# The output projection of a two-block layer on one core: plain products, and products of block sums for 12 of 16 feature tiles

## The chip, the cores and the metric

The kernel runs on one core of one Trainium2 chip. The metric is the device time of one execution in microseconds. PE is TensorE's matmul side, PEld its weight loads, DVE is VectorE, ACT is ScalarE, POOL is GpSimd and SP is SyncE, which here only issues DMAs.

## The reference, cut to what matters

Two blocks follow each other on x of 512 positions by 2048 features (batch 1). The first is a mixer of attention and a gated recurrence; the second has three attention branches, each brought up to 2048 features, gated and summed. The change touches only the last line:

```
merged = g_a * (oa @ w_up_a) + g_b * (ob @ w_up_b) + g_c * (oc @ w_up_c)
x = x + merged @ w_o          # (512 x 2048) @ (2048 x 2048)
```

## The kernel before

All activations are held transposed: features on the 128 partitions in 16 tiles (KT = 16), the 512 positions along the free side. A product is one output tile of 128 features by 512 positions, summed over the 16 input tiles in one bank. float32 accuracy comes from splitting both operands in two fp32r parts, hi (a rounded copy) and lo (what is left): each input tile takes three matmuls, hi by hi (L824), weight hi by activation lo (L825), weight lo by activation hi (L826), each 128x128 weights by 512 columns.

**Weights** come in items of up to 1024 columns (`weights()`, 438 of them, ITEMS). SP loads item after item into a ring of three buffers `wraw` (L2255), ACT makes `whi` (`split`, L1125), POOL makes `wlo` (`remainder`, L2127), and PE's `part` waits for it. `w_o` gives 32 items, two for each output tile (input tiles 0 to 7 and 8 to 15, LOW and HIGH).

**Order.** Every engine runs the same walk, `in_order`, over its own program, so each engine's instructions stand in the order of that walk. `Beat` has three lines of side work ("core", "post", "slow"): each line holds generators, and each slot (one after four input tiles of a part) lets each line take one step. `drain` takes steps until the named lines are empty, with no matmul of a part between them.

**The last stages.** `mix(2, 6)` makes the merged activations: for each output tile nb a gate (16 input tiles), then a short product over six tiles (`thin`), then on DVE the evacuation `bank * gate` (L1711) and the sum with the other two branches (L1715) into `y[nb]`, which counts `mg2`. A gate's own side work is three ACT functions, one on DVE (L1742), one on ACT and a copy on POOL (L2185). Beside it `put` makes hi (ACT, L1262) and lo (DVE L1659 for three of four tiles, POOL L2145 for the fourth) of each finished `y[k]`; these are the moving operands "m" of the last product. Tiles 0 to 7 are ready when the last product begins, tiles 8 to 15 follow beside its first 96 matmuls (two output tiles' LOW halves stand first for that). For each output tile SP loads `x1s[nb]` (`out_load`, L2366), DVE adds bank and `x1s` (L1722, `kind == "last"`), and SP stores the result (L2352). The last tile is evacuated in two halves of 256 columns, the second stored from ACT's queue.

Of the kernel before, what the change touches and what calls it, by code (L numbers as in the profile page):

```python
# [97 lines left out]
def weights():  # L98
# [159 lines left out]
class Memory:  # L258
    def __init__(self, nc, ctx):
# [112 lines left out]

        self.cmb = {1: self.cmb[:, 0:256], 2: self.rt[1], 3: self.cmb}

    def dst(self, kind, i=0, *_):
# [36 lines left out]
class Signals:  # L412
    def __init__(self, nc, ctx):
# [56 lines left out]

        self.u, self.ua, self.mg2, self.out = sem("u"), sem("ua"), sem("mg2"), sem("out")


# [8 lines left out]
def in_order(beat, do):  # L482
# [170 lines left out]
    def mx(k):  # L653
        return "m", k, "y", k, ("mg2", k + 1), k % 4 != 0

    def mx_early():
        beat.add("slow", puts(*([mx(k)] for k in range(EARLY, 8))))

    for nb, _ in enumerate(mix(2, 6)):
        if nb < EARLY:  # L660
            beat.add("slow", puts([], [], [mx(nb)]))
    beat.drain("core", "post", "slow")
    beat.add("slow", puts(*([mx(k), mx(k + 1)] for k in range(8, 16, 2))))
    do["out_load"](0)
    do["out_load"](1)
    second = (beat.open(), beat.open())
    for n, ks in enumerate((LOW, HIGH)):
        for nb, bank in enumerate(second):
            do["part"]("m", ks, bank, n == 0, n == 1)
            if n:  # L670
                close("last", bank, nb)
    for nb in range(2, KT):
        do["out_load"](nb)
        full("m", "last", nb)
    do["end"]()
# [41 lines left out]
def tensor_program(nc, M, S, beat):  # L717
# [115 lines left out]
    def out(kind, bank, *at):  # L833
        if kind in BY_ACT:
            free[bank] = (S.eva, n.up("eva"))
        elif kind in BY_DVE:
            free[bank] = (S.evd, n.up("evd"))
        else:
            free[bank] = {"x1": (S.x1, n["x1"] + 1), "mix": (S.u, n["mix"] + 1), "last": (S.out, n["last"] + 1)}[kind]
# [258 lines left out]
    def h2(k):  # L1098
        put("h", k, None, 0, None, on_vector(k))

    in_order(beat, dict(
        setup=setup, mem=mem, mem_kv=nothing, mem_norm=lambda: rest(3), mem_turn=mem_turn, ada=nothing, h=h,
        begun=begun, hv=hv, gates=lambda g: rest(GATE_STEPS), hg=hg, attend=attend, window=window, put=put, x_load=nothing, h2=h2, index=index,
        topk=lambda: rest(48), mix_load=nothing, out_load=nothing, end=nothing,
        part=part, out=out, posts=dict(
# [6 lines left out]
def scalar_program(nc, io, M, S, beat):  # L1112
# [144 lines left out]
    def put(x, k, src, i, mark, on_dve):  # L1257
        act.wait_ge({"y": S.y, "o": S.o, "mg2": S.mg2, "nrm": S.nrm}[mark[0]], mark[1])
        act.wait_ge(S.item, beat.used[home(x, k) if home(x, k)[0] != "t" else ("o", 5)])
        if x == "y" and home(x, k)[0] == "o":  # L1260
            act.wait_ge(S.adm, 2 * KT)
        e.activation(M.pair[x][0][k], src[i] if isinstance(src, list) else {"y": M.y, "ost": M.ost}[src][i],  # L1262
                     ACT.Copy).then_inc(S.phi)

    def out(kind, bank, *at):
# [12 lines left out]
        if kind == "x1":  # L1278
# [3 lines left out]
            e.activation(M.sqt if i else M.sqa, M.y[nb], ACT.Square).then_inc(S.xsqa)  # L1282
        if kind == "last" and at[0] == KT - 1:
            act.wait_ge(S.out, KT + 1)
            e.dma_start(io["out"][KT - 1, :, LAST[1]], M.u[1][:, LAST[1]]).then_inc(S.ust[1], 16)
        if kind == "ik":
# [237 lines left out]
    def h2(k):  # L1524
        act.wait_ge(S.x1, NB.index(k) + 1)
        act.wait_ge(S.item, beat.used["h", k])
        e.activation(M.pair["h"][0][k], M.y[k], ACT.Copy, scale=M.c("norm_g2", k, 1)).then_inc(S.phi)

    def nothing(*at):
        pass  # L1530
# [3 lines left out]
        gates=lambda g: rest(GATE_STEPS), hg=hg, attend=attend, window=window, put=put, x_load=nothing, h2=h2, index=index, topk=lambda: rest(48), mix_load=nothing,  # L1534
        out_load=nothing, end=nothing, part=part, out=out, posts=dict(
            decay=decay, hq=silu("hq"), hz=silu("hz"),
# [10 lines left out]
def vector_program(nc, M, S, beat):  # L1547
# [128 lines left out]
    def out(kind, bank, *at):  # L1676
# [28 lines left out]
        elif kind == "mix":  # L1705
# [6 lines left out]
            if branch == 2:  # L1712
                dve.wait_ge(S.u, 32 + nb + 1)
                dve.wait_ge(S.lb[nb % 2], 16 * (8 + nb // 2 + 1))
                e.tensor_tensor(M.y[nb], M.u[nb % 2], M.lb[nb % 2], ALU.add).then_inc(S.mg2)  # L1715
        elif kind == "last":
            nb = at[0]
            dve.wait_ge(S.lb[nb % 2], 16 * (16 + nb // 2 + 1))
            dve.wait_ge(S.ust[nb % 2], 16 * (16 + nb // 2))
            dve.wait_ge(S.item, beat.item)  # L1720
            for w in LAST if nb == KT - 1 else (slice(0, T),):
                e.tensor_tensor(M.u[nb % 2][:, w], src[:, w], M.lb[nb % 2][:, w], ALU.add).then_inc(S.out)  # L1722

# [372 lines left out]
    def h2(k):  # L2096
# [6 lines left out]
        else:  # L2103
            n.up("plp")

    def nothing(*at):
        pass

    in_order(beat, dict(
        setup=setup, mem=mem, mem_kv=nothing, mem_norm=mem_norm, mem_turn=lambda: rest(2), ada=ada, h=h, begun=begun, hv=nothing,  # L2110
        gates=gates, hg=hg, attend=attend, window=window, put=put, x_load=nothing, h2=h2, index=index, topk=topk, mix_load=nothing, out_load=nothing, end=nothing,
        part=part, out=out, posts=dict(
# [6 lines left out]
def gpsimd_program(nc, M, S, beat):  # L2119
# [106 lines left out]
    def h2(k):  # L2226
        phi = n.up("phi")
        if not on_vector(k):
            pool.wait_ge(S.phi, phi)
            pool.wait_ge(S.hb, [nb for nb in NB if not on_vector(nb)].index(k) + 1)  # L2230
            e.tensor_tensor(M.pair["h"][1][k], M.hb[k], M.pair["h"][0][k].bitcast(F32), ALU.subtract).then_inc(S.plp)  # L2231

    def nothing(*at):
        pass

    def idle(steps):
# [11 lines left out]
def sync_program(nc, io, M, S, beat):  # L2248
# [90 lines left out]
    def out(kind, bank, *at):  # L2339
        if kind == "x1":  # L2340
            i, nb = at
            sp.wait_ge(S.x1, i + 1)
            e.dma_start(io["x1s"][nb], M.y[nb]).then_inc(S.x1s, 16)
        elif kind == "mix" and at[0] < 2:
            branch, nb = at
            sp.wait_ge(*((S.u, nb + 1) if branch == 0 else (S.ua, nb + 1)))
            e.dma_start(io["mgs"][nb], M.u[nb % 2]).then_inc(S.ust[nb % 2], 16)
        elif kind == "last":
            nb = at[0]
            sp.wait_ge(S.out, nb + 1)  # L2350
# [11 lines left out]

    def out_load(nb):
        sp.wait_ge(*((S.out, nb - 1) if nb > 1 else (S.mg2, 16)))
        sp.wait_ge(S.x1s, 16 * KT)
        e.dma_start(M.lb[nb % 2], io["x1s"][nb]).then_inc(S.lb[nb % 2], 16)  # L2366

    def end():
        for b in range(2):
            sp.wait_ge(S.ust[b], 16 * (24 + b))  # L2370

# [3 lines left out]
    def idle(steps):  # L2375
# [4 lines left out]
        gates=gates, hg=hg, attend=attend, window=window,  # L2380
        put=nothing, x_load=x_load, h2=nothing, index=idle(3), topk=idle(48), mix_load=mix_load, out_load=out_load,
        end=end, part=part, out=out, posts=dict(
# [110 lines left out]
```

## Time and profile before

| | us |
|---|---|
| median of three runs | 2596.74 (2596.69 to 2596.79) |
| the profiled execution | 2597.67 |
| its span, first to last instruction | 2596.4 |
| busy: PE / PEld / DVE / ACT / POOL | 2580.0 / 2077.6 / 1028.8 / 1082.6 / 1140.5 |

The page gives busy time of each engine, the chain of waits followed back from the last instruction (97% PE, 3% DVE), and groups of instructions by line. A row of the timeline reads: start in us from the span's start, duration in us, engine, line, operation, output<-input, count, and in brackets the idle time before and what ended it. A matmul's duration runs to its modelled end, and the next begins before that: the pace is read from starts.

### The profile page before, as it was taken

The page shows a single profiled execution, that of the slowest core. Times are in us where ns is not written, and L with a number is a line of the kernel's source. Part 1 is how long each engine was busy: PE and PEld are TensorE (multiplying, and loading weights), DVE is VectorE, ACT ScalarE, POOL GpSimd, SP SyncE. Part 2 cuts the span into 40 slices and gives each one's busy share as a digit, 9 for nine tenths or more (in the row PEclk, how much of TensorE's full clock was granted, in tenths as well). Part 3 has the DMA queues.
Part 4 walks back from the last instruction along what each step waited for, and adds up shares of the span by engine and source line. Part 5 has one row for each costly group of instructions (what it writes and reads, how often), then busy time and mean ns, then how long its engine had stood idle before and what let it go on. Part 6 is the DMA issues. An engine that isn't in the chain of part 4 may idle for free.

```text
span 2596.4 us, 33094 instructions
## 1 busy us (share of the span) xinstructions
PE 2580.0 (99%) x13414; PEld 2077.6 (80%) x13414; DVE 1028.8 (40%) x1622; ACT 1082.6 (42%) x1769; POOL 1140.5 (44%) x580
## 2 busy tenths in 40 slices
PE   8999999999999999999999999999999999999999
PEld 3778777877888888888888888888888888888887
DVE  3963444435444421344785343334333223312300
ACT  4334344444445432344444444444444444333311
POOL 0014444343434454543454444445555556554543
PEclk9999999999999999999999999999999999999999
DMA  9953333233333244422222333333333333333443
GB/s 398 389 176 111 106 99 113 82 118 102 122 102 114 86 134 146 126 89 81 90 81 86 106 99 100 103 100 106 102 107 119 120 110 111 119 108 115 148 145 104
DMA packets 97785, 322.84 MB, mean 124 GB/s; under 512 B 10977, under 2 KB 13025, under 8 KB 93025
## 3 DMA queue, kind: packets, MB, share of 16 engines
q1 hardware_dynamic: 92016, 301.16, 34.9%
q10 hardware_dynamic: 5616, 19.56, 2.0%
q8 instruction: 107, 1.75, 0.3%
q14 instruction: 46, 0.37, 0.0%
HBM read 303.90 MB, written 16.78 MB: 124 GB/s over the span
## 4 chain that ended last, share of the span: by engine, by line
PE 97%; DVE 3%; DMA 0%; ACT 0%; issue 0%; POOL 0%; SPq 0%; DVEq 0%; ACTq 0%
PE bank L824 28%; PE bank L826 28%; PE bank L825 28%; PE bank L767 2%; PE bank L1019 1%; PE bank L1008 1%; PE bank L939 1%; DVE TA L1610 1%; PE bank L1002 1%; PE bank L973 1%; DVE first L1610 1%; DVE wlo L1593 0%; PE bank L1055 0%; PE bank L1070 0%; PE bank L788 0%; PE bank L866 0%
## 5 line engine op out<-in xcount | busy, mean ns | idle before, releaser
L2127 POOL TENSOR_TENSOR wlo<-wraw,whi 128x1024 fp32r<-128x1024 f32 (+3 forms) x420 | 970.2, 2310 | 1318.4 <-ACT whi L1125 1318.2
L824 PE MATMUL bank<-Hhi,whi 128*128 128x512 f32 x2720 | 1093.6, 402 | 0.2 <-POOL Hlo L2231 0.2
L826 PE MATMUL bank<-Hhi,wlo 128*128 128x512 f32 x2720 | 1061.9, 390 | 0.0
L825 PE MATMUL bank<-Hlo,whi 128*128 128x512 f32 x2720 | 1060.5, 390 | 0.0
L1125 ACT ACTIVATE whi<-wraw 128x1024 fp32r<-128x1024 f32 (+3 forms) x438 | 440.5, 1006 | 685.9 <-PE bank L826 647.2
L824 PEld LDWEIGHTS bank<-Hhi,whi 128*128 128x128 f32 x2720 | 511.0, 188 | 113.8 <-issue 9.9
L826 PEld LDWEIGHTS bank<-Hhi,wlo 128*128 128x128 f32 x2720 | 510.6, 188 | 109.2
L825 PEld LDWEIGHTS bank<-Hlo,whi 128*128 128x128 f32 x2720 | 511.4, 188 | 103.5 <-issue 2.2
L824 PE MATMUL bank<-Ohi,whi 128*128 128x512 f32 x320 | 127.9, 400 | 0.0
L826 PE MATMUL bank<-Ohi,wlo 128*128 128x512 f32 x320 | 124.8, 390 | 0.0
L825 PE MATMUL bank<-Olo,whi 128*128 128x512 f32 x320 | 124.6, 389 | 0.0
L1689 DVE TENSOR_TENSOR TA<-bank,rows 128x512 f32<-128x512 f32 x48 | 33.1, 690 | 201.7 <-PE bank L826 201.7
L1795 DVE TENSOR_TENSOR TR<-TA,TR 128x512 fp32r<-128x512 f32 x38 | 51.2, 1347 | 77.5 <-ACT TR L1352 77.5
L1742 DVE SCALAR_TENSOR_TENSOR TA<-TA,par 128x512 f32<-128x512 f32 x48 | 46.7, 972 | 71.7 <-ACT TA L1302 69.2
L1742 DVE SCALAR_TENSOR_TENSOR TA<-TA 128x512 f32<-128x512 f32 x32 | 60.1, 1879 | 33.3 <-ACT TA L1302 33.3
L1722 DVE TENSOR_TENSOR TA<-bank,TA 128x512 f32<-128x512 f32 (+1 forms) x17 | 11.1, 660 | 151.6 <-PE bank L826 151.6
L824 PEld LDWEIGHTS bank<-Ohi,whi 128*128 128x128 f32 x320 | 60.1, 188 | 13.3 <-issue 1.4
L825 PEld LDWEIGHTS bank<-Olo,whi 128*128 128x128 f32 x320 | 60.1, 188 | 13.1 <-issue 1.2
L826 PEld LDWEIGHTS bank<-Ohi,wlo 128*128 128x128 f32 x320 | 60.1, 188 | 12.6
L1274 ACT ACTIVATE TA<-bank 128x512 f32<-128x512 f32 x49 | 29.0, 592 | 97.2 <-PE bank L826 97.2
L1689 DVE TENSOR_TENSOR Y<-bank,rows 128x512 f32<-128x512 f32 x45 | 30.9, 687 | 92.7 <-PE bank L826 86.1
L767 PE MATMUL bank<-wmem,HF 128*128 128x512 f32 x128 | 59.6, 617 | 8.1 <-ACT HF L1156 8.1
(272 smaller groups left out, 2733.9 us busy)
## 6 DMA issues: line engine op xcount, KB each, us to landing
wraw<-in_w_in SPq DMA_DIRECT2D x293, 512.0 KB, 3.5
TA<-in_w_ada SPq DMA_DIRECT2D x22, 1024.0 KB, 17.1
first<-in_w_ada SPq DMA_DIRECT2D x32, 512.0 KB, 4.5
wraw<-in_w_out SPq DMA_DIRECT2D x32, 512.0 KB, 3.5
wraw<-in_w_o SPq DMA_DIRECT2D x32, 512.0 KB, 3.5
first<-in_w_ada SPq DMA_DIRECT2D x10, 1024.0 KB, 14.0
wmem<-in_w_mem ACTq DMA_DIRECT2D x16, 512.0 KB, 9.4
wraw<-in_w_beg ACTq DMA_DIRECT2D x16, 512.0 KB, 7.7
```

The lines of the kernel that those rows point to most:

```text
L767: m = e.matmul(M.banks[MEM_BANKS[2 * kv + tt]], M.memf[k][:, tt * P:(tt + 1) * P], w[:, kv * T:(kv + 1) * T], start=k == 0, stop=k == KT - 1)
L824: e.matmul(out, hi[:, c], xhi[k], start=first and j == 0, stop=False)
L825: e.matmul(out, hi[:, c], xlo[k], start=False, stop=False)
L826: m = e.matmul(out, lo[:, c], xhi[k], start=False, stop=last and end)
L939: m = e.matmul(M.banks[bank][keys:keys + G, i * w:(i + 1) * w], k[:, i * P + keys:i * P + keys + G], q[:, i * P + queries:i * P + queries ...
L1125: e.activation(M.whi[b][:, 0:w], M.wraw[b][:, 0:w], ACT.Copy).then_inc(S.hi)
L1274: e.activation(M.dst(kind, *at), src, ACT.Copy).then_inc(S.eva)
L1610: e.tensor_tensor_reduce(out=w, in0=w, in1=M.cb, scale=gain, scalar=begin, op0=ALU.mult, op1=ALU.add, accum_out=total).then_inc(S.adv)
L1689: e.tensor_tensor(dst, src, M.rows, ALU.mult).then_inc(S.evd)
L1742: e.scalar_tensor_tensor(out=M.t2, in0=x, scalar=bias, in1=M.t1, op0=ALU.min, op1=ALU.subtract).then_inc(S.t2)
L1795: e.tensor_tensor(M.sql, M.W2["SQ"], M.sqh.bitcast(F32), ALU.subtract).then_inc(S.sql)
L2127: e.tensor_tensor(M.wlo[b][:, 0:w], M.wraw[b][:, 0:w], M.whi[b][:, 0:w].bitcast(F32), ALU.subtract).then_inc(S.lo)
```

## The change

Input tiles are paired, six pairs (`CROSSED`: 0 and 1, 2 and 3, 4 and 5, 10 and 11, 12 and 13, 14 and 15), output tiles are paired (8 groups), and positions are halved (LEFT, RIGHT, 256 each). Each two by two block product is made in seven products of block sums in place of eight. The four input tiles 6 to 9 (`PLAIN`) stay plain, n1 and n2, 12 matmuls of 512 columns each; a product is 18 matmuls of 256 columns. The order is `SEQ`; the plain parts of group g + 1 stand ahead of the products of group g.

- Sums of activations: four DVE operations of 256 columns for each pair (`sums`), hi of 256, 512 and 1024 columns on ACT, lo of 256 and 512 on POOL and of 1024 on DVE (`forms`).
- Sums of weights: p5, p6, p7 and p3 each need a DVE sum of 768 columns (`low`), then hi of 768 columns on ACT (`high`), then lo: on DVE for p1, p5, p6, p7, p3, on POOL for p2, p4, n1, n2. All are made three products ahead (LOOK), in four buffers.
- Banks: p1, p6, p7, p4 accumulate in one bank R; after each DVE takes the running sum (`take`, 256 columns, bank and SBUF in), and PE waits for that before the next of them. p5 and p3 do so in Q. p2 adds to the plain sum in X. DVE ends a group with two additions of 512 columns.
- DVE, in a step of product q, first takes product q - 1, then makes what product q + 3 needs.
- The last plain weights no longer pass through the ring; `begin` makes the first three hi and lo after the walk's last `thin`, behind `forms(4)`. SP issues four 768-column loads, two 512-column loads, two `x1s` loads and two stores for each group, in place of four 1024-column loads, two `x1s` loads and two stores.
- `w_o` is laid out anew by the host, in the order of the tiles.

```diff
+CROSSED = ((0, 1), (2, 3), (4, 5), (10, 11), (12, 13), (14, 15))
+PLAIN = range(6, 10)
+STRIP = len(CROSSED) * P
+PRODUCTS = ("p1", "p5", "p6", "p2", "p7", "p3", "p4")
+SEQ = [(0, "n1"), (0, "n2")]
+for pair in range(GROUPS):
+    SEQ += [(pair + 1, x) for x in ("n1", "n2") if pair < GROUPS - 1] + [(pair, x) for x in PRODUCTS]
+LO_BY_POOL = ("n1", "n2", "p2", "p4")
+LOOK = 3
...
     def mx_early():
-        beat.add("slow", puts(*([mx(k)] for k in range(EARLY, 8))))
+        beat.add("slow", do["forms"](3))
+        beat.add("slow", puts([mx(6), mx(7)], [mx(8), mx(9)]))
+        beat.add("slow", do["begin"]())
+        beat.add("core", rest(2))
+        beat.add("core", do["sums"](4))
+        beat.add("core", do["forms"](4))
...
     beat.drain("core", "post", "slow")
...
+    beat.add("slow", do["sums"](5))
+    beat.add("slow", do["forms"](5))
+    beat.drain("slow")
+    for q in range(len(SEQ)):
+        do["last"](q)
...
# PE
+    def last(q):
+        pe.wait_ge(S.lop if what in LO_BY_POOL else S.lod, lows(q, what in LO_BY_POOL))
...
+        elif what in ("p1", "p5"):
...
+                pe.wait_ge(S.took, 6 * g - (what == "p5"))
+        elif what != "p2":
+            pe.wait_ge(S.took, 6 * g + {"p6": 1, "p3": 2, "p7": 3, "p4": 4}[what])
...
+            e.matmul(out, hi[:, c], xhi, start=start and j == 0, stop=False, skip_group_check=True)
+            e.matmul(out, hi[:, c], xlo, start=False, stop=False, skip_group_check=True)
+            m = e.matmul(out, lo[:, c], xhi, start=False, stop=True, skip_group_check=True)
...
# ACT
+        if q == 0:
+            act.wait_ge(S.lo, len(ITEMS))
...
+        else:
+            act.wait_ge(S.item, len(ITEMS) + q - 3)
+        if what in ("p5", "p6", "p7", "p3"):
+            act.wait_ge(S.wsum, 4 * g + ("p5", "p6", "p7", "p3").index(what) + 1)
...
+        e.activation(M.hi4[q % 4][:, 0:at.shape[-1]], at, ACT.Copy).then_inc(S.hi)
...
# DVE
+        elif what == "p7":
+            e.tensor_tensor(a21, a21, a11, ALU.add).then_inc(S.wsum)
...
+        e.tensor_tensor(lo, src, M.hi4[q % 4][:, 0:STRIP].bitcast(F32), ALU.subtract).then_inc(S.lod)
...
+        elif what == "p6":
+            e.tensor_tensor(x1[:, RIGHT], R, x1[:, RIGHT], ALU.add).then_inc(S.took)
...
+    def last(q):
+        if q:
+            take(q - 1)
+        low(q + LOOK)
```

## Rows read from the trace of the kernel before

**Rows 1.** Windows view, the last product: us, then busy time (instructions) of each engine.

```profile
core 0: us, PE busy (x) PEld busy (x) DVE busy (x) ACT busy (x) POOL busy (x), PEclk, DMA share, GB/s
2419.30:2593.60 174.30, 174.30 (x770) 144.07 (x768) 21.74 (x24) 35.99 (x38) 76.46 (x33) 1.00 0.41 131
```

**Rows 2.** Timeline, two L824 matmuls of 512 columns, three matmuls apart.

```profile
2479.92 0.39 PE L824 MATMUL bank<-Hhi,whi 128*128 128x512 f32 x1
...
2480.60 0.39 PE L824 MATMUL bank<-Hhi,whi 128*128 128x512 f32 x1
```

**Rows 3.** Timeline, two fp32r matmuls of 256 columns and the one behind them.

```profile
1230.22 0.28 PE L1088 MATMUL bank<-Olo,Ohi 128*128 128x256 f32 x1
...
1230.34 0.28 PE L1089 MATMUL bank<-Olo,Ohi 128*128 128x256 f32 x1
...
1230.45 0.40 PE L824 MATMUL bank<-Hhi,whi 128*128 128x512 f32 x1
```

**Rows 4.** Timeline, twenty weight loads of 128 columns with short matmuls between them.

```profile
240.43 2.42 PEld L973 LDWEIGHTS bank<-TA,Y 128*128 128x128 f32 x20
```

**Rows 5.** Source view, DVE: duration min/median/max in ns, first and last start, forms.

```profile
L1593 DVE TENSOR_TENSOR wlo<-wraw,whi x18: 1218/1222/1226, 71.2 to 165.6; 128x1024 fp32r<-128x1024 f32 x18
L1659 DVE TENSOR_TENSOR Hlo<-Y,Hhi x13: 678/1092/2234, 913.2 to 2431.1; 128x512 fp32r<-128x512 f32 x13
L1711 DVE TENSOR_TENSOR TA<-bank,TA x48: 683/692/693, 1412.4 to 2420.2; 128x512 f32<-128x512 f32 x48
L1722 DVE TENSOR_TENSOR TA<-bank,TA x17: 415/692/693, 2436.0 to 2594.1; 128x512 f32<-128x512 f32 x15, 128x256 f32<-128x256 f32 x2
```

**Rows 6.** Lines view by form: ACT's hi of 768 columns.

```profile
L1125 ACT ACTIVATE whi<-wraw 128x768 fp32r<-128x768 f32 x32 | 27.0, 845 | 47.1 <-PE bank L826 47.1
```

**Rows 7.** Source view, POOL's lo of 512 columns, and of weights from 1700 us on.

```profile
L2145 POOL TENSOR_TENSOR TR<-Y,TR x1: 1296/1296/1296, 2274.9 to 2274.9; 128x512 fp32r<-128x512 f32 x1
...
L2127 POOL TENSOR_TENSOR wlo<-wraw,whi x172: 732/2399/2902, 1698.6 to 2578.6; 128x1024 fp32r<-128x1024 f32 x125, 128x768 fp32r<-128x768 f32 x32, 128x256 fp32r<-128x256 f32 x12, 128x512 fp32r<-128x512 f32 x3
```

**Rows 8.** Timeline, POOL: a copy of 512 columns, and the lo of 768.

```profile
2403.62 0.61 POOL L2185 COPY TA<-TA 128x512 f32<-128x512 f32 x1
2406.98 1.85 POOL L2127 TENSOR_TENSOR wlo<-wraw,whi 128x768 fp32r<-128x768 f32 x1 [2.75 <-ACT whi L1125]
```

**Rows 9.** Timeline, POOL and DVE side by side.

```profile
2416.72 2.41 POOL L2127 TENSOR_TENSOR wlo<-wraw,whi 128x1024 fp32r<-128x1024 f32 x1 [1.67 <-ACT whi L1125]
2417.05 2.62 DVE L1715 TENSOR_TENSOR Y<-TA 128x512 f32<-128x512 f32 x1
```

**Rows 10.** Timeline, an item's last matmul and those who waited for it.

```profile
2484.45 0.39 PE L826 MATMUL bank<-Hhi,wlo 128*128 128x512 f32 x1
...
2484.94 1.06 ACT L1125 ACTIVATE whi<-wraw 128x1024 fp32r<-128x1024 f32 x1 [4.38 <-PE bank L826]
2484.98 0.69 DVE L1722 TENSOR_TENSOR TA<-bank,TA 128x512 f32<-128x512 f32 x1 [10.19 <-PE bank L826]
...
2486.08 2.40 POOL L2127 TENSOR_TENSOR wlo<-wraw,whi 128x1024 fp32r<-128x1024 f32 x1 [3.04 <-ACT whi L1125]
```

**Rows 11.** Timeline near the start: ACT hands to DVE, and DVE to a waiting PE.

```profile
76.95 0.72 ACT L1239 ACTIVATE Hhi<-Y,par 128x512 fp32r<-128x512 f32 x1 [6.57 <-DVE Y L1616]
...
77.71 0.75 DVE L1630 SCALAR_TENSOR_TENSOR Hlo<-Y,par,Hhi 128x512 fp32r<-128x512 f32 x1 [0.79 <-ACT Hhi L1239]
...
78.56 0.47 PE L788 MATMUL bank<-whi,Hhi 128*128 128x512 f32 x1 [1.16 <-issue]
```

**Rows 12.** Timeline ahead of the last product and its first matmul.

```profile
2414.41 0.61 ACT L1262 ACTIVATE Hhi<-Y 128x512 fp32r<-128x512 f32 x1
...
2419.40 0.39 PE L824 MATMUL bank<-CKhi,whi 128*128 128x512 f32 x1
```

**Rows 13.** Timeline, the last evacuation.

```profile
2593.78 0.76 DVE L1722 TENSOR_TENSOR TA<-bank,TA 128x256 f32<-128x256 f32 x2 [10.19 <-PE bank L826]
```

**Rows 14.** DMA view: KB each, median us from issue to landing.

```profile
wraw<-in_w_o SPq DMA_DIRECT2D x32, 512.0 KB, 3.5
```

More of the change, by code:

```diff
@@ L838, in out @@
         else:
-            free[bank] = {"x1": (S.x1, n["x1"] + 1), "mix": (S.u, n["mix"] + 1), "last": (S.out, n["last"] + 1)}[kind]
+            free[bank] = {"x1": (S.x1, n["x1"] + 1), "mix": (S.u, n["mix"] + 1)}[kind]
             n.up(kind)
@@ L1103, in tensor_program @@
         begun=begun, hv=hv, gates=lambda g: rest(GATE_STEPS), hg=hg, attend=attend, window=window, put=put, x_load=nothing, h2=h2, index=index,
[L1104 removed]
+        topk=lambda: rest(48), mix_load=nothing, end=nothing, sums=lambda j: rest(1), forms=lambda j: rest(2),
+        begin=lambda: rest(3), last=last,
         part=part, out=out, posts=dict(
@@ L1534, in scalar_program @@
         gates=lambda g: rest(GATE_STEPS), hg=hg, attend=attend, window=window, put=put, x_load=nothing, h2=h2, index=index, topk=lambda: rest(48), mix_load=nothing,
-        out_load=nothing, end=nothing, part=part, out=out, posts=dict(
+        end=nothing, sums=lambda j: rest(1), forms=forms, begin=begin, last=last,
+        part=part, out=out, posts=dict(
             decay=decay, hq=silu("hq"), hz=silu("hz"),
@@ L1713, in out @@
                 dve.wait_ge(S.u, 32 + nb + 1)
+                if nb == 14:
+                    dve.wait_ge(S.fd, 4)
                 dve.wait_ge(S.lb[nb % 2], 16 * (8 + nb // 2 + 1))
                 e.tensor_tensor(M.y[nb], M.u[nb % 2], M.lb[nb % 2], ALU.add).then_inc(S.mg2)
[L1716 to L1722, printed above, removed]
     def gates(g):
@@ new lines, in last @@
+    def last(q):
+        if q == 0:
+            x1_load(0)
+            x1_load(1)
+            sp.wait_ge(S.fp, 8)
+            sp.wait_ge(S.fd, 4)
+            sp.wait_ge(S.item, len(ITEMS) + 1)
+            for what in ("a21", "a22", "a12"):
+                block(0, what)
+            a_blocks(1)
+            n_blocks(2)
+        elif q > 2 and SEQ[q][0] and SEQ[q] == (SEQ[q][0], "p1"):
+            g = SEQ[q][0]
+            store(g - 1)
+            if g < GROUPS - 1:
+                x1_load(g + 1)
+                a_blocks(g + 1)
+            if g < GROUPS - 2:
+                n_blocks(g + 2)
+        if q == len(SEQ) - 1:
+            store(GROUPS - 1)
@@ L2380, in sync_program @@
         gates=gates, hg=hg, attend=attend, window=window,
-        put=nothing, x_load=x_load, h2=nothing, index=idle(3), topk=idle(48), mix_load=mix_load, out_load=out_load,
+        put=nothing, x_load=x_load, h2=nothing, index=idle(3), topk=idle(48), mix_load=mix_load, sums=idle(1), forms=forms,
+        begin=idle(3), last=last,
         end=end, part=part, out=out, posts=dict(
```

320 lines of the change are left out of this document (280 added, 40 removed).

## Prediction

> **What bounds the kernel now.** I read the windows view over the last product first, then PE's timeline inside it, then the durations of every kind of operation that the change adds, wherever the trace has one. In the last product PE is busy for all of its 174.30 us, at full granted clock, while DVE is busy for 21.74, ACT for 35.99 and POOL for 76.46 [rows 1]. The pace of a 512-column matmul is (2480.60 - 2479.92) / 3 = 0.2267 us [rows 2], so 768 of them are 174.1 us. No other engine shows there; fewer columns on PE is the way to less time, until another engine's chain is longer than PE's.
>
> **What PE saves.** A group (two output tiles) has 96 matmuls of 512 columns now: 21.76 us. Afterwards it has 24 of 512 columns (5.44 us) and 7 x 6 x 3 = 126 of 256. Two such, each with its own weight load, took 1230.45 - 1230.22 = 0.23 us [rows 3]: 0.115 each. Bounds: 256 columns at 2.4 GHz are 0.107; adding what a 512-column matmul takes over its own 0.213, 0.013, gives 0.120. A row of twenty weight loads ran at (2.42 - 0.19) / 19 = 0.117 [rows 4], 0.19 being one load, so the load does not rule 0.115 out, and 0.115 is measured on the very form. A product is then 18 x 0.115 = 2.07 us, a group 5.44 + 14.49 = 19.93, all eight 159.4: 14.7 us under now. A group breaks even at (21.76 - 5.44) / 126 = 0.1295.
>
> One page of the Trainium skill speaks against it: TensorE: Matmul & The Clock Gate, section "The mechanism", says that a weight load overlaps matmuls in flight only where their row groups differ. By that rule, every load of this kernel would lie bare. [Rows 3] show full-height loads hidden even under 256 columns, so it has next to no weight in the sum.
>
> **What DVE, ACT and POOL now have to do in step with PE.** Prices: a DVE operation on two SBUF tiles is 0.69 us for 512 columns and 1.22 for 1024 [rows 5], so 0.96 for 768; a take of 256 columns 0.42, an addition from a bank of 512 columns 0.69 [rows 5]; independent DVE operations overlap by 2 x 0.42 - 0.76 = 0.08 [rows 13]. ACT's hi of 768 is 0.85 [rows 6], POOL's lo 1.85 for 768 and 1.30 for 512 [rows 8, 7]. ACT to DVE is 0.04, and I take 0.03 to 0.04 for the way back; a waiting PE starts 0.10 after DVE's end, and its first matmul is 0.08 longer [rows 11]. DVE starts 0.14 after an item's last matmul ends [rows 10]; with 0.28 for a 256-column matmul [rows 3] that is 0.30 after the next product has begun.
>
> DVE's work per group is 9 x 0.96 + 6 x 0.42 + 2 x 0.69 = 12.5 us of 19.9, not a bound by share. But p6, p7, p3 and p5 each want sum, hi, lo in turn (0.96 + 0.03 + 0.85 + 0.03 + 0.96 = 2.83), and DVE stands still while ACT makes hi. PE may not begin p7 before DVE has taken p6 out of bank R, and in DVE's order that take stands behind the weights of p3. From the end of p1: take p1 starts at 0.30, sum of p7 0.64 to 1.60, hi to 2.48, lo to 3.47, take p5 to 3.81, sum of p3 3.73 to 4.69, hi to 5.57, lo to 6.56, take p6 to 6.90, PE at 7.00. PE itself needs 3 x 2.07 = 6.21 for p5, p6, p2. PE waits 0.79, with the longer first matmul 0.87, in each of eight groups.
>
> **The port.** DVE operations with two SBUF inputs range from 0.68 to 2.23 us, those that read a bank from 0.683 to 0.693 [rows 5]; a 0.69 one that began 0.33 after a POOL operation took 2.62 and ended 0.54 after it [rows 9]. I read that as: such an operation and a POOL operation take turns. In the chain, hi of p2 follows that of p6; counted from the group's start (0.30, take p4 0.42, addition 0.03 + 0.69, two rounds of 0.88 + 0.91 + 0.96) lo of p6 ends at 6.9, POOL's lo of p2 runs from there to 8.7, and the sum of p7 wants to start at 5.44 + 2.07 + 0.64 = 8.15. It waits 0.55. So p7 waits 1.42 in seven groups (the last has no plain parts in its walk, DVE is ahead there by one turn, 0.87): 10.8 us. Bounds: nothing, or the whole 1.85 instead of 0.55, 9 us more.
>
> **The last group** has no plain parts between p4 of group 6 and its own p1. Three products ahead, DVE makes p5 (from 0.3 after p3 of group 6 began: take, sum, hi, lo to 3.5), takes p3 (0.3), adds 512 columns (0.7), makes p6 (2.7), and only then takes p4, 7.5 us after p3 began, when PE has been done for 7.5 + 0.1 - 4.14: 3.6 us with the restart.
>
> **The start.** The first plain lo, POOL's, stands behind lo of m7, the gate's copy, lo of m9 and two of `forms(4)`. The m conversions stand where ACT now converts at 2414.41 [rows 12]; hi of m7 ends about 1.1 later, POOL starts at 2415.6 and needs 4 x 1.30 + 0.73 + 0.61 = 6.5 [rows 7, 8]: 2422.1, where PE is free at 2419.40 [rows 12]. That is 2.8 with the hand-over; DVE's m8 and y15 take turns with it, at most 2 x 0.69 and one 1.22 more. I take 3.7, between 2.8 and 5.4; nothing excludes less if ACT comes earlier. The four plain parts (10.9 us) cover `sums(5)` and `forms(5)`; DVE is then about 0.7 late at the first take, added once. During `mix` the new sums stand beside a PE that needs 15 us per tile (66 matmuls), and 2.9 us of DVE and 2.1 of ACT for each pair of tiles are hidden there; if they are not, it shows as idle PE before 2419.
>
> **DMA.** The weights' bytes are the same and x and output too, 131 GB/s now [rows 1]; a 512 KB load lands 3.5 us after issue [rows 14], and each block is issued most of a group ahead. Free; SP waits only for steps that lie behind. If the first group's three blocks, issued after the first plain part, were later than 10 us, p5 would wait.
>
> **The end.** The last evacuation is one of 0.42 in place of two in 0.76 [rows 13]: -0.35.
>
> **Sum.** 159.4 + 10.8 + 3.6 + 0.7 + 3.7 = 178.2 against 174.1: +4.1, at the end -0.35: +3.8. On the profiled execution's 2597.67 that is 2601.5; the median of the runs is 0.93 below it, so I forecast 2600.5. A nanosecond of pace is worth only 0.4 us, since DVE's chain stays: 0.107 to 0.120 gives -3.3 to +2.0.
>
> **Rivals.**
> - *DVE keeps up*: the chain to p7 is 7.0 against 6.2, a matter of ten hand-overs and five durations interpolated or taken elsewhere. If they overlap better, p7 waits little, the start costs 1.5, and what is left is 159.4 + 3.6 + 1.5 = 164.5: about 2587. For it: DVE's share of 63%. Against: every term has its row, and the order is strict.
> - *The port decides (slower)*: POOL has four passes a group, 6.3 us, and any that starts ahead of a sum or lo in p7's chain adds up to 1.85. It makes the change slower by 0.2% once it adds 0.2 us more to a group than I count; a full pass gives 3.8 + 7 x 1.3 = +13: 2610. For it: DVE waits of 2 us at 512 columns in [rows 5, 9]. Against: in my order POOL's lo of p4, n1 and n2 falls where DVE is idle.
> - *The load sets the pace*: 126 loads in a row at 0.130 make +5.6 on the stage where I have -0.4: +10, 2606. [Rows 4], at 0.117, speak against.
> - *Loads not hidden in a long row*: 0.115 + 0.117 [rows 3, 4] for each of 1008 matmuls, with 43.5 for the plain ones 277 in place of 174: 2700. [Rows 3] leave it a chance of 1%. It is what the rule of the Trainium skill's page TensorE: Matmul & The Clock Gate, section "The mechanism", would make of this stage.
>
> **Chances.** The forecast's case 0.46, DVE keeps up 0.25, port 0.20, pace 0.08, unhidden 0.01. 0.2% is 5.2 us, about what a measurement of this kernel can tell from no change. The forecast's case has 0.36 within it, 0.08 above and 0.02 below; the first rival is faster, the others slower: 0.27, 0.36, 0.37. Its own range is 2595 to 2606; the range over all cases 2586 to 2611.
>
> **What would show it.** Right: starts of 256-column matmuls 0.113 to 0.118 apart; seven gaps on PE of about 1.4 us ahead of p7, released by DVE's take; one of 3.6 late; one of some 3.7 at 2419, released by POOL. In DVE's rows sums of 0.96, some stretched by 0.5. Wrong: no idle PE at p7 (then the first rival), DVE operations near 2.8 us (the second), a pace over 0.12 (the third), or waits for DMAs.

## The result and the profile after

The changed kernel takes 2611.17 us (median of four runs, 2610.45 to 2612.29) beside 2596.76 for the kernel before on the same chip: a ratio of 1.0055, with a 95% interval of 1.0043 to 1.0067. That is 14.4 us more, 0.55%, where 3.8 more were forecast; it lies 0.2 us above the range and on its slow side. The profiled execution took 2610.45, its span is 2609.1, so between the two profiled spans there are 12.7 us. The runs of the changed kernel spread over 1.8 us, those of the kernel before over 0.3.

The page's head, each engine's busy time and instructions:

```profile
span 2609.1 us, 34342 instructions
PE 2576.8 (99%) x13846; PEld 2094.0 (80%) x13846; DVE 1135.1 (44%) x1762; ACT 1107.2 (42%) x1815; POOL 1132.0 (43%) x590
```

PE is busy for only 3.2 us less than the 2580.0 of before, in a longer span, and DVE for 106 more. The windows view over the last product shows where. The rows are the start, the middle, the last group's first 8 us and the whole stage:

```profile
core 0: us, PE busy (x) PEld busy (x) DVE busy (x) ACT busy (x) POOL busy (x), PEclk, DMA share, GB/s
2418.50:2431.00 12.50, 8.87 (x27) 6.74 (x27) 10.73 (x8) 4.30 (x8) 10.52 (x9) 0.73 0.38 119
2447.00:2585.00 138.00, 130.57 (x948) 123.80 (x949) 80.00 (x107) 42.16 (x55) 39.95 (x25) 1.00 0.40 134
2585.00:2593.00 8.00, 4.52 (x27) 4.35 (x26) 3.80 (x6) 1.58 (x2) 1.93 (x1) 0.79 0.17 66
2418.70:2606.90 188.20, 171.17 (x1202) 160.77 (x1200) 113.13 (x144) 55.71 (x74) 57.94 (x37) 0.97 0.37 124
```

Beside [rows 1] there are three new things. PE idles: 17 us of the stage. The granted clock is not 1.00 any more at two places, 0.73 at the start and 0.79 in the last group. And PE is busy for 171.17 where the forecast's own matmuls came to 159.4 (a busy time holds the modelled ends and the slow matmuls too). The stage takes 187.9, from 2418.77 (behind the last matmul of `mix`) to 2606.7, in place of 174.1.

**The pace.** PE's timeline inside p2 of group 1:

```profile
2466.18 0.28 PE L1199 MATMUL bank<-TR,w3lo 128*128 128x256 f32 x1
...
2466.54 0.28 PE L1199 MATMUL bank<-FX,w3lo 128*128 128x256 f32 x1
```

Three matmuls take 0.36: 0.120 each, and that is what most of the 1008 show. [Rows 3] had 0.115.

**The wait ahead of p7**, the same stretch of all engines: DVE makes the sum of p3 (L2295), ACT its hi, DVE its lo (L2300) and only then takes p6 (L2318).

```profile
2465.68 0.95 DVE L2295 TENSOR_TENSOR first<-first 128x768 f32<-128x768 f32 x1
...
2466.72 1.58 ACT L1662 ACTIVATE whi<-first 128x768 fp32r<-128x768 f32 x2 [2.35 <-DVE first L2295]
...
2467.62 0.28 PE L1199 MATMUL bank<-Hlo,w3lo 128*128 128x256 f32 x1
2467.67 0.96 DVE L2300 TENSOR_TENSOR wlo<-first,whi 128x768 fp32r<-128x768 f32 x1 [1.04 <-ACT whi L1662]
...
2468.55 0.42 DVE L2318 TENSOR_TENSOR TA<-bank,TA 128x256 f32<-128x256 f32 x1
...
2469.11 0.36 PE L1197 MATMUL bank<-TR,whi 128*128 128x256 f32 x1 [1.21 <-DVE TA L2318]
```

From 2467.62 to 2469.11 are 1.49, less one step of pace 1.37, and 0.08 more for the longer first matmul. DVE stood still for 1.04 between its sum and its lo, 0.84 for hi and 0.20 for the two hand-overs. Six groups are like this; the first waits 2.12 and the last 0.77. Why DVE is behind is told by the source views of its sum for p7 (L2291) and of the take:

```profile
L2291 DVE TENSOR_TENSOR first<-first x4: 948/1562/1570, 2461.9 to 2593.5; 128x768 f32<-128x768 f32 x4
```

```profile
L2318 DVE TENSOR_TENSOR TA<-bank,TA x8: 416/418/419, 2446.5 to 2599.6; 128x256 f32<-128x256 f32 x8
...
  PE bank L1197: 9.9, 8
```

The sum takes 1.56 where POOL's lo of p2 runs beside it, and 0.948 in the last group, where nothing does. PE waited for the take 8 times.

**The two long waits and what stands behind them.** The start:

```profile
2418.54 0.39 PE L891 MATMUL bank<-Ohi,wlo 128*128 128x512 f32 x1
2422.56 0.80 PE L1197 MATMUL bank<-Hhi,w3hi 128*128 128x512 f32 x1 [3.63 <-POOL w3lo L2492]
2423.15 0.63 PE L1198 MATMUL bank<-Hlo,w3hi 128*128 128x512 f32 x1
2423.58 0.63 PE L1199 MATMUL bank<-Hhi,w3lo 128*128 128x512 f32 x1
```

A wait of 4.02 - 0.23 = 3.79, released by POOL. Then the matmuls begin 0.43 apart in place of [rows 2]'s 0.227: the 1.2 GHz level. That goes on for 13 of them, 2.9 us in all.

The last group:

```profile
2585.64 0.28 PE L1199 MATMUL bank<-Hhi,w3lo 128*128 128x256 f32 x1
...
2588.84 0.41 DVE L2333 TENSOR_TENSOR TA<-TA,bank 128x256 f32<-128x256 f32 x1
...
2589.40 0.55 PE L1197 MATMUL bank<-TR,whi 128*128 128x256 f32 x1 [3.48 <-DVE TA L2333]
...
2590.18 0.41 PE L1197 MATMUL bank<-TR,whi 128*128 128x256 f32 x1
```

A wait of 3.76 - 0.12 = 3.64, and 13 matmuls of 256 columns, most of them 0.213 apart, 1.4 us more. Here the Trainium skill's page TensorE: Matmul & The Clock Gate has a section, "HAM oscillation — how this bites in real kernels", by which a wait inside a kernel can put TensorE back to half its clock, so that the work behind it starts slow; these rows agree, and the prediction had no term for it.

The whole stage is then 1008 x 0.120 + 192 x 0.2267 = 164.5 for the matmuls, 2.20 + 6 x 1.46 + 0.85 = 11.8 for the waits ahead of p7, 3.8 and 3.6 for the two long ones, 2.9 + 1.4 = 4.3 for the clock: 188.0, where 187.9 were measured.

**What sets the time at the start.** That sum says what PE did, not what each part of it cost. The critical view, which follows the work that ended last, leaves PE for 28 us here: it goes from the last matmul of `mix` to DVE, through DVE's and ACT's operations one behind the other, and comes back to PE with p7 of the first group.

```profile
2418.70 0.24 PE bank L891
2419.03 0.70 DVE TA L1858
...
2446.54 0.43 DVE TA L2318
2447.11 0.36 PE bank L1197
```

In all that time DVE waits only for ACT (five times 1.0 to 1.1), never for PE. Several of its operations are long beside POOL's: 2.29 and 1.87 for lo of 1024 and 768 columns and 2.27 for the sum of p7, which take 1.23, 0.96 and 0.95 elsewhere in the stage. So the wait of 3.79, the 2.9 us of slow matmuls behind it and the first group's pace did not lengthen this execution: without them PE would have waited for the same take for longer. In the last group it is otherwise. There the same view goes through the slow matmuls of p1, and their 1.4 us count.

### The profile page after: what moved, and what is told of

Same layout as the page of the kernel before. It is cut to its first block, busy times and chain, and to the rows that moved or that the text cites. A ratio compares the mean times of both kernels' runs of the same rounds, so it can differ in the third digit from the quotient of the medians.

```text
span 2609.1 us, 34342 instructions
## 1 busy us (share of the span) xinstructions
PE 2576.8 (99%) x13846; PEld 2094.0 (80%) x13846; DVE 1135.1 (44%) x1762; ACT 1107.2 (42%) x1815; POOL 1132.0 (43%) x590
## 4 chain that ended last, share of the span: by engine, by line
PE 94%; DVE 4%; ACT 1%; issue 1%; DMA 0%; POOL 0%; DVEq 0%; SPq 0%; ACTq 0%
PE bank L889 26%; PE bank L891 25%; PE bank L890 25%; PE bank L832 2%; PE bank L1084 1%; PE bank L1073 1%; PE bank L1197 1%; PE bank L1199 1%; PE bank L1198 1%; PE bank L1004 1%; DVE TA L1757 1%; PE bank L1067 1%; PE bank L1038 1%; DVE first L1757 1%; ACT whi L1662 1%
## 5 line engine op out<-in xcount | busy, mean ns | idle before, releaser
L2370 POOL TENSOR_TENSOR wlo<-wraw,whi 128x1024 fp32r<-128x1024 f32 (+3 forms) x388 | 894.6, 2306 | 1218.9 <-ACT whi L1227 1218.8
L889 PE MATMUL bank<-Hhi,whi 128*128 128x512 f32 x2544 | 1025.1, 403 | 0.2 <-POOL Hlo L2474 0.2
L891 PE MATMUL bank<-Hhi,wlo 128*128 128x512 f32 x2544 | 993.4, 390 | 0.0
L890 PE MATMUL bank<-Hlo,whi 128*128 128x512 f32 x2544 | 992.1, 390 | 0.0
L1227 ACT ACTIVATE whi<-wraw 128x1024 fp32r<-128x1024 f32 (+3 forms) x406 | 406.5, 1002 | 554.4 <-PE bank L891 515.5
L889 PEld LDWEIGHTS bank<-Hhi,whi 128*128 128x128 f32 x2544 | 477.9, 188 | 106.9 <-issue 9.9
L891 PEld LDWEIGHTS bank<-Hhi,wlo 128*128 128x128 f32 x2544 | 477.5, 188 | 102.4
L890 PEld LDWEIGHTS bank<-Hlo,whi 128*128 128x128 f32 x2544 | 478.3, 188 | 96.8 <-issue 2.2
L1465 ACT ACTIVATE TA<-bank,par 128x512 f32<-128x512 f32 x39 | 26.9, 689 | 97.4 <-PE bank L932 97.4
## 6 DMA issues: line engine op xcount, KB each, us to landing
TA<-in_w_ada SPq DMA_DIRECT2D x22, 1024.0 KB, 17.1
```

The costliest lines, as they stand in the source:

```text
L889: e.matmul(out, hi[:, c], xhi[k], start=first and j == 0, stop=False)
L890: e.matmul(out, hi[:, c], xlo[k], start=False, stop=False)
L891: m = e.matmul(out, lo[:, c], xhi[k], start=False, stop=last and end)
L1227: e.activation(M.whi[b][:, 0:w], M.wraw[b][:, 0:w], ACT.Copy).then_inc(S.hi)
L1465: e.activation(W["R"], M.bST, ACT.Ln, scale=1.0 / k, bias=M.eps).then_inc(S.ln)
L2370: e.tensor_tensor(M.wlo[b][:, 0:w], M.wraw[b][:, 0:w], M.whi[b][:, 0:w].bitcast(F32), ALU.subtract).then_inc(S.lo)
```

## The experiments

The theory when the runs were planned, by PE's own sum: against the forecast, 5 us come from a pace of 0.120, which is PE's own in a long row, and 4.3 from the clock that falls behind PE's waits of over 3 us; the waits themselves are as priced. (That the first 2.9 of the 4.3 lie beside DVE's chain was not in it.) Rivals: the pace is 0.115 and something around (ports, DVE, POOL) makes it 0.120; the slow matmuls belong to the kernel's start and end, or to its new form, and not to the waits.

**Pace alone.** The kernel before, each of its last product's matmuls cut in two of 256 columns; its DVE, ACT, POOL and DMA work stays. This kernel does not compute the right product: both halves of a bank are begun with `start`, and its output is off by 0.177, about what the first input tile missing from one half would give (an estimate, the root of 1/32; which terms are missing was not shown). Number and shape of PE's matmuls are as said, and the reading rests on those.

```diff
-            e.matmul(out, hi[:, c], xhi[k], start=first and j == 0, stop=False)
...
+            for w in (slice(0, 256), slice(256, 512)) if x == "m" else (slice(0, T),):
+                begins = first and j == 0
+                e.matmul(out[:, w], hi[:, c], xhi[k][:, w], start=begins, stop=False, skip_group_check=True)
...
```

> The kernel before, with each group of three matmuls of the last product made for 256 columns and then for the other 256, weights loaded anew for each: 1536 matmuls of 256 columns with nothing else changed and nothing to wait for. Theory (a long row of such matmuls runs at 0.120 each, the pace that the changed kernel shows): the stage is 1536 x 0.120 = 184.3 us in place of 174.1: +10.2, 2607. Rival (0.115 to 0.116, the pace of the isolated pairs before, and 0.120 is what DVE's and POOL's work beside it makes of it): 177.4: +3.3, 2600.

Measured: 2607.59 (2607.11 to 2607.62), ratio 1.0040 (1.0024 to 1.0056). Windows view, and PE's timeline:

```profile
2440.00:2580.00 140.00, 140.00 (x1169) 140.00 (x1168) 8.30 (x12) 25.48 (x24) 57.51 (x25) 1.00 0.41 136
```

```profile
2500.00 0.28 PE L826 MATMUL bank<-CKhi,whi 128*128 128x256 f32 x1
...
2500.36 0.28 PE L826 MATMUL bank<-CKhi,whi 128*128 128x256 f32 x1
```

No wait, full clock, 0.120 per matmul with DVE busy for 6% of the time. POOL is busy for 41% of it, but the starts are 0.120 apart where POOL stands idle as well as beside its operations. So the pace is that of the row itself, and the rival of 0.115 falls. 1536 matmuls at 0.120 are 184.3, 10.2 over 174.1; the run is 10.4 over its control.

**The order on DVE.** In every group the take of p6 is put ahead of lo of p3.

```diff
-        low(q + LOOK)
+        if SEQ[q][1] == "p2":
+            low(q + LOOK - 1, (1,))
+        low(q + LOOK, (0,) if SEQ[q][1] == "p6" else (0, 1))
...
```

The second argument of `low` names its steps: 0 is the sum, 1 is the lo.

> The changed kernel, with DVE's lo of p3 moved behind its take of p6; nothing else. Theory (p7's wait is DVE's order: the take stands behind work that PE needs only two products later): the seven gaps of 1.38 us and the one of 2.1 ahead of p7 go, with the 0.08 of each restart; -10.5: 2600.7. Rival (the port: POOL's lo of p2 keeps the sum of p7 waiting): gaps of at least 0.6 stay ahead of p7, -6 at most: 2605.

Measured: 2600.59 (2599.72 to 2602.27, ten runs), ratio 1.0013 (1.0004 to 1.0023). 10.6 us of the 14.4 are gone. PE's windows row has 133.86 busy of 135; what is left is the first group's wait, 1.30:

```profile
2440.00:2575.00 135.00, 133.86 (x987) 127.94 (x987) 84.49 (x112) 45.12 (x59) 41.65 (x26) 1.00 0.41 137
```

So the order made those waits, as the prediction's chain had it. In the last group the wait has grown from 3.64 to 4.6, since PE now comes there earlier than DVE does:

```profile
2580.31 0.55 PE L1197 MATMUL bank<-TR,whi 128*128 128x256 f32 x1 [4.46 <-DVE TA L2337]
```

**The port.** Only 8 of 768 columns of p2's lo are made, so that POOL is out of the way of p7's sum; PE makes the same matmuls, with what the buffer held before in the other 760.

```diff
-        w = src.shape[-1]
+        w = src.shape[-1] if what != "p2" else 8
+        src = src[:, 0:w]
```

> The changed kernel, with POOL's lo of p2 made for 8 of 768 columns in every group, so that the rest of that lo is left out of the result's terms; order and waits unchanged. Theory (DVE's sum of p7 stands still while POOL makes lo of p2): the sum of p7 takes 0.96 in place of 1.56, and each gap ahead of p7 shrinks by 0.6: seven groups, -4: 2607. Rival (no turn-taking, the 1.56 has another cause): the gaps stay at 1.38, 2611.

Measured: 2606.87 (2606.43 to 2607.11), ratio 1.0038 (1.0023 to 1.0052). Source view of the sum, and a wait ahead of p7:

```profile
L2291 DVE TENSOR_TENSOR first<-first x4: 948/949/950, 2462.1 to 2589.5; 128x768 f32<-128x768 f32 x4
```

```profile
2467.84 0.28 PE L1199 MATMUL bank<-Hlo,w3lo 128*128 128x256 f32 x1
2468.71 0.36 PE L1197 MATMUL bank<-TR,whi 128*128 128x256 f32 x1 [0.60 <-DVE TA L2318]
```

The sum is back at 0.949, by 0.61, and the wait falls from 1.38 to 0.76, by 0.62. DVE and POOL do take turns, and each turn that stands in p7's chain reaches PE in full. The Trainium skill's page SBUF — State Buffer, section "Who interferes with whom", has this rule (an operation with two SBUF inputs against a POOL operation that reads SBUF: one blocks), and the trace agrees, 0.6 a group.

The first group shows it more strongly. There the sum of p7 falls from 2.27 to 0.95, and p7 begins 1.30 us earlier (2445.81 for 2447.11). Something else stands there too: behind a wait of only 1.95 ahead of that p7, 15 matmuls ran slow, beginning 1.5 us after the wait's end.

**The start.** `begin`'s first plain lo is put ahead of `forms(4)` in the walk.

```diff
+        def first_of_begin():
+            yield
+            next(begin)
+            yield
...
-        beat.add("core", rest(2))
+        beat.add("core", first_of_begin())
```

> The changed kernel, with the first plain lo (and its hi) made one slot of the gate's HIGH half earlier, ahead of m7, m9 and forms(4) in POOL's order. Theory (POOL's queue makes the start wait, and the wait lets TensorE's clock fall): the 3.8 us gap ahead of the first matmul goes, the granted clock in 2418 to 2431 stays at 1.0 in place of 0.73, the plain matmuls are 0.227 apart and not 0.427; 6.7 us are won there, and some 1.5 given back as waits for lo of n2 and for forms(5): 2611.2 - 5.2 = 2606. Rival (the low clock comes with the change of stage, new banks and new operands, and not with the gap): the gap goes, the first 13 matmuls still stand 0.427 apart: 2609.

Measured: 2610.18 (2609.54 to 2612.16), ratio 1.0050 (1.0033 to 1.0067): 1 us less than the changed kernel, which is within the spread of the runs, and 4 more than expected. The wait of 3.8 is gone and the matmuls behind it run at 0.227, but POOL has the same passes to make and is late for the next two plain products:

```profile
2421.53 0.39 PE L1206 MATMUL bank<-Hhi,w3lo 128*128 128x512 f32 x1
2422.91 0.50 PE L1204 MATMUL bank<-Hhi,whi 128*128 128x512 f32 x1 [0.98 <-POOL wlo L2499]
...
2428.27 0.39 PE L1206 MATMUL bank<-Hhi,wlo 128*128 128x512 f32 x1
2431.66 0.79 PE L1204 MATMUL bank<-Hhi,whi 128*128 128x512 f32 x1 [3.00 <-POOL wlo L2499]
```

1.15 and 3.16. Behind 1.15 the matmuls stay at full pace; behind 3.16 they are slow again, in another place and another group than in the changed kernel. A wait on a queue that is full was moved, not removed. And it could not have given 5 us: p7 of the first group began at 2446.48 in place of 2447.11, again after a wait for DVE's take, of 1.98. Most of those 0.6 us was lost again in the last group, where in this execution 28 matmuls ran slow behind the wait of 3.64, for 2.8 us.

**The last group.** DVE takes p4 of group 6 ahead of what it makes for p6 of group 7.

```diff
-        if q:
+        if q and SEQ[q] != (GROUPS - 1, "p1"):
             take(q - 1)
+        if SEQ[q] == (GROUPS - 2, "p4"):
+            take(q)
```

> The changed kernel, with DVE's take of p4 of group 6 moved ahead of the weights of p6 of group 7; nothing else. Theory (the wait of 3.64 us ahead of p1 of group 7 is this order, and the clock falls behind it): a gap of some 0.8 stays, and the 14 matmuls that ran 0.1 longer run at full clock: -2.8 - 1.5 = -4.3: 2606.9. Rival (the slow matmuls after the gap are not from the gap): -2.8: 2608.4.

Measured: 2611.34 (2610.07 to 2611.42), ratio 1.0052 (1.0037 to 1.0067): nothing gained where 4.3 were expected. The wait ahead of p1 fell to 0.78, but DVE's work was only put off, and PE met it at p7:

```profile
2596.41 0.28 PE L1199 MATMUL bank<-Hlo,w3lo 128*128 128x256 f32 x1
2599.53 0.36 PE L1197 MATMUL bank<-TR,whi 128*128 128x256 f32 x1 [2.85 <-DVE TA L2318]
...
2600.26 0.41 PE L1199 MATMUL bank<-CKhi,wlo 128*128 128x256 f32 x1
2600.48 0.41 PE L1197 MATMUL bank<-cbr,whi 128*128 128x256 f32 x1
```

A wait of 3.0, and 0.6 us behind its end the pace goes from 0.12 to 0.21.

This trace also differs from the changed kernel's in a place that the edit does not touch. At the start only 7 matmuls ran slow and PE came to the first group's p7 1.2 us earlier (2443.63 for 2444.87). It gained nothing by it: DVE's take stands where it stood, and so does p7.

```profile
2446.54 0.42 DVE L2318 TENSOR_TENSOR TA<-bank,TA 128x256 f32<-128x256 f32 x1
...
2447.10 0.55 PE L1197 MATMUL bank<-TR,w3hi 128*128 128x256 f32 x1 [3.20 <-DVE TA L2318]
```

The wait is 3.35 in place of 2.12, and behind it 12 matmuls ran slow, 1.3 us, which the changed kernel's trace does not have. So some of what the edit may have gained is hidden by the clock's own spread, and what it is worth by itself is not settled by this run.

**All three together.**

> The three moves together. Theory: what is left of the stage is PE at 0.120 per 256-column matmul, 164.5 us, with some 3 us of small waits: 2611.2 - 5.2 - 10.5 - 4.3 = 2591.2, under the 2596.8 of the kernel before. Rival (with PE ahead by that much, DVE's chain of p5, p6, p7 and p3 shows somewhere else in each group, as waits for lo or for the takes): gaps of about 1 us per group come back elsewhere: 2599.

Measured: 2596.44 (2595.72 to 2598.49, ten runs), ratio 0.9997 (0.9988 to 1.0006): no slower and no faster than the kernel before, and 5 above what was expected. The start still has its 1.15 and 3.16 and the slow matmuls behind, and the last group waits of 1.75 and 1.0. Windows, the start and the middle:

```profile
2418.50:2440.00 21.50, 17.52 (x85) 14.33 (x84) 16.99 (x15) 6.55 (x10) 12.64 (x9) 0.92 0.55 201
2440.00:2575.00 135.00, 134.87 (x995) 128.91 (x994) 84.30 (x113) 45.12 (x59) 40.50 (x25) 1.00 0.41 137
```

With take and lo exchanged and less lost in the last group, the middle has no wait left but 0.13.

**The fourth plain lo early too**, on top of these three, made before the sums and forms of the last pair:

```diff
+        high(3)
+        yield
...
     def last(q):
-        high(q + LOOK)
+        if q:
+            high(q + LOOK)
...
```

That is ACT's part; POOL's is the same with `low`.

> The three moves together, and the hi and lo of n2 of group 1 made ahead of sums and forms of the last pair. Theory (the 3.2 us wait ahead of n2 of group 1 and the clock's fall behind it come from that order): both go, 3.2 + 1.8 us, and up to 1.6 come back as a wait for lo of p1: 2596.4 - 3.4 = 2593.0, below the kernel before by more than noise. Rival (DVE's late sums of the last pair only move the wait to p1, and it stays above 3 us there with the clock's fall): 2596.

Measured: 2596.15 (2595.38 to 2597.74, eleven runs), ratio 0.9997 (0.9988 to 1.0006). The wait of 3.16 and the clock's fall are gone:

```profile
2418.50:2440.00 21.50, 18.02 (x99) 14.98 (x98) 17.49 (x15) 6.40 (x10) 12.12 (x9) 1.00 0.57 201
2440.00:2575.00 135.00, 133.26 (x980) 127.14 (x978) 84.33 (x114) 45.12 (x59) 40.51 (x25) 1.00 0.41 137
2575.00:2595.00 20.00, 15.57 (x126) 15.22 (x126) 11.97 (x18) 4.01 (x5) 3.91 (x2) 1.00 0.15 53
```

But DVE, 17.5 of 21.5 us busy at the start, is now late for products of the first group: seven waits of 0.6 to 1.8 stand in the stage, five up to 2444.23 and two in the last group, 8.2 us in all. Expected was 2593. By the critical view the chain at the start runs through DVE and ACT from 2419.2 to 2444.2, where p7 of the first group begins; that is 0.5 us earlier than with the three moves alone (2444.23 for 2444.75). The wait of 3.16 and the 1.7 us of slow matmuls behind it are gone, and only those 0.5 us have come of it.

**Waits of several lengths, and nothing else.** The kernels above show slow matmuls only behind waits, but in each the surroundings changed too. So: the kernel before, PE held back ahead of six of its output tiles until DVE has made the evacuation of the tile before, 1 to 6 times over.

```diff
+HELD = {3: 1, 5: 2, 7: 3, 9: 4, 11: 5, 13: 6}
...
+            if kind == "last" and at[0] in HELD:
+                pe.wait_ge(S.out, at[0] + 1)
...
+            for _ in range(HELD.get(nb, 1) - 1):
+                e.tensor_tensor(M.u[nb % 2], src, M.lb[nb % 2], ALU.add).then_inc(S.held)
+                dve.wait_ge(S.held, n.up("held"))
```

> The kernel before, in which PE may not begin output tile 4, 6, 8, 10, 12 or 14 of the last product until DVE's evacuation of the tile ahead of it is done, and in which DVE makes that evacuation 1, 2, 3, 4, 5 and 6 times over, one after the other. Nothing else of the work changes, so PE stands idle six times, 21.8 us apart, with no short matmul and no new weights near. Each idle time should be 0.16 + 0.14 + 0.10 for ending, taking and starting again, and 0.69 for the first and some 0.73 for each further evacuation: 1.1, 1.8, 2.6, 3.3, 4.0 and 4.7 us, 17.5 in all. Theory (a long idle time costs the clock, whatever it comes from): behind 3.3, 4.0 and 4.7 the next dozen matmuls of 512 columns stand 0.427 apart in place of 0.227, some 2.6 us each, behind 1.1 and 1.8 none do, and 2.6 tells on which side it lies: 2597.2 + 17.5 + 7.9 = 2622.6 (2625 if 2.6 counts too). Rival (the slow matmuls of the changed kernel come from what surrounds the waits there, its weights, its POOL passes or its 256 columns): the waits alone, 2614.7.

Measured: 2621.86 (2619.97 to 2622.73), ratio 1.0096 (1.0079 to 1.0113). The windows view of the 3.2 us behind each wait, in order; the last number but two is the granted clock:

```profile
2463.80:2467.00 3.20, 3.13 (x14) 2.55 (x15) 0.02 (x1) 0.34 (x1) 2.40 (x1) 1.00 0.59 188
2487.50:2490.70 3.20, 3.12 (x14) 2.57 (x15) 0.02 (x1) 0.00 (x0) 2.09 (x1) 1.00 0.58 175
2511.90:2515.10 3.20, 3.12 (x14) 2.58 (x15) 0.03 (x1) 0.00 (x0) 1.35 (x1) 1.00 0.65 198
2537.00:2540.20 3.20, 3.11 (x8) 2.49 (x9) 0.04 (x1) 0.00 (x0) 0.62 (x1) 0.58 0.72 213
2564.50:2567.70 3.20, 3.16 (x8) 2.50 (x9) 0.00 (x0) 0.00 (x0) 0.00 (x0) 0.55 0.73 224
2592.60:2595.80 3.20, 3.11 (x8) 2.49 (x9) 0.04 (x1) 0.00 (x0) 0.00 (x0) 0.54 0.48 164
```

By starts, the waits were 1.04, 1.77, 2.49, 3.21, 3.94 and 4.67. Behind the first three 14 matmuls began in 3.2 us, behind the others 8. The falls behind the last three cost 1.7, 1.7 and 1.5 us by the steps over 0.227, less than the 2.6 each that I had put down from the changed kernel's start. That the time came within 1 us of the 2622.6 expected is in part luck: the falls gave 3.0 us less, and behind the last matmul the kernel took 1.2 us longer (4.3 for 3.15), for which there is no cause here. PE's part is clear by itself: the last matmul comes 22.4 us later than in the kernel before, 17.1 from the waits, 4.9 from the falls and the rest from restarts. The theory holds, and the rival, at 2614.7, falls: no new weights, 256-column matmuls or POOL passes are needed for it.

## Why the prediction was wrong

The forecast named the waits ahead of p7, in the last group and at the start, with their releasers. The steps that failed are in its sum: it put the start's terms one behind the other on PE, where DVE's chain alone sets the time and is longer; it took 5 ns too little for the pace and 0.13 us too little for each pair of hand-overs; and it had no term for the clock.

- **The start: wrong path, mis-sized.** The forecast puts the first group's p7 at 3.7 + 10.9 + 4 x 2.07 + 1.34 + 0.7 = 24.9 us after the stage's start (1.34 is its 1.42 without the restart); it began 28.3 after it, 3.4 later. The wait for POOL was 3.8 for 3.7, but it set nothing. What sets the time is what the prediction has as "DVE is then about 0.7 late at the first take": DVE's operations took longer beside POOL's, 3.3 us in the three named above alone. The prediction had such turns only in its bounds for POOL's wait and in p7's sum.
- **What PE saves: mis-sized.** "0.115 is measured on the very form" took two matmuls between others for a row of a thousand. The row runs at 0.120, the upper bound that the text had worked out as 0.107 + 0.013. The stage's matmuls are 164.5, not 159.4: +5.1. Not all of it reaches the time. Where PE then waits for DVE's chain, its slower pace only shortens that wait: that holds for the first 72 matmuls, for p5, p6 and p2 of seven groups and for p3 and p4 of group 6. It leaves 522 x 5 ns = 2.6.
- **"A nanosecond of pace is worth only 0.4 us": a slip.** 54 of a group's 126 matmuls lie beside DVE's chain. Their 0.43 us per ns over eight groups is what comes back out of the waits; the other 72 of each group make 0.58.
- **The chain ahead of p7: mis-sized.** At 0.120 the forecast's wait of 1.42 would have been 1.42 - 54 x 5 ns = 1.15; it was 1.46. A pair of hand-overs took 0.20, where [rows 11] had given 0.07, twice in the chain: 0.26. The sum of p7 took 1.56, not 0.96 + 0.55 = 1.51. That is the whole 0.31, in six groups 1.9. The two chains of the last group, to its p1 and to its p7, each have two such pairs as well and are longer by 0.2 to 0.3 each: 0.5.
- **Missing: what long waits do to the clock.** Two waits of over 3 us were forecast and priced at their own length. PE's slow matmuls behind them are 2.9 and 1.4 us. The first 2.9 lie beside DVE's chain and cost nothing here; the second cost 1.3 over the 0.08 of a restart.
- **The last group's wait:** 3.6 measured, 3.6 forecast, with the releaser that was named; that it is right hides a chain 0.3 longer and a PE 0.2 later.
- **DMA, hidden loads:** no wait of PE for either; free, as said. The stage begins 0.63 us earlier than [rows 12] have it, and the end gains 0.5 where 0.35 was said.

3.4 + 2.6 + 1.9 + 0.5 + 1.3 are 9.7, where the stage is 9.8 longer than forecast. Less 0.63 and 0.15 that makes 8.9 to 9.0, which is what lies between the 3.8 forecast and the spans' 12.7. The shares of the start and of the pace are worked out from the chain in the traces. Two runs bear on the start: PE coming 1.2 us earlier did not move p7, and the sum of p7 1.32 us shorter moved it by 1.30. The other long operations of DVE there were not tested one by one. The medians differ by 1.7 more than the spans do. The lengths of the slow stretches differ between executions of one form (13 slow matmuls here, 6 to 9 behind an equal wait in other kernels), which would spread the runs; that this is the whole of the 1.7 was not shown.

Of the rivals, *the port decides* named 2610, but not as it happened: its extra 1.3 a group is not there in the middle. In the first group it was nearer than the forecast, since DVE's turns with POOL are what made that chain long. That the number lies near is in good part luck. *The load sets the pace* had a slower pace, with 0.130 for 0.120. *DVE keeps up* was never open at 2587: with the true pace the matmuls alone leave 9.6 us to gain, and the two kernels in which DVE nearly keeps up stand at 2596.

## What to carry over

A pace for a form that will run a thousand times has to be taken from a long row of it, or the upper bound taken: here 5 ns too few were 5.1 us of a forecast saving of 14.7. Terms of one engine may be added only where that engine is on the chain: at the start PE's wait, its slow matmuls and its pace cost nothing, since DVE's own chain from the stage's start to the first take of p6 was longer. In these kernels a wait of PE of three us or more brought 1.3 to 2.9 us of slow matmuls on top of its length; short ones, with one exception, only their length. Whether that reaches the time is to be asked again by the chain. Where the queue that releases PE is full at that point (POOL and DVE at the start, DVE in the last group), reordering moves the wait; only in the middle, where DVE had 40% to spare, did it remove it.

## What was not expected of the hardware

- A matmul of 512 columns takes 0.2267, two of 256 with a weight load each 0.240, with nothing else changed.
- The clock fell behind every wait of 3.0 us or more (3.0, 3.15, 3.16, 3.21, 3.35, three of 3.64, four of 3.8, 3.94, 4.6, 4.67), and, in the kernel of held waits, not behind 1.04, 1.77 and 2.49. Once, with p2's lo cut to 8 columns, 15 slow matmuls stood 1.5 us behind a wait of only 1.95, while 1.98 and 2.12 at the same place in other kernels had none; why was not settled.
- The fall can come late, and not by the wait's length: behind 3.64 it came at once in two executions and 1.5 us late in a third; 0.6 to 0.7 us late behind 3.0 and 3.21; at once behind 4.67. The slow stretch is as uneven: 1.3 us and 2.8 us behind the same wait of 3.64.
- A matmul behind a wait is followed 0.07 to 0.11 late even where the clock holds.
